# Query and key projections of a head as seven half-size products, with their weight sums on GpSimd and VectorE

## The reference, cut to what matters

```python
h = rms_norm(x, norm_mix)
proj = h @ w_in                       # queries, keys, values, z of 16 heads, and more
qkv_c = silu(causal_depthwise_conv(qkv_buf, qkv, dn_conv_w))
q, k, v = (t.reshape(b, l, DN_HEADS, DN_HEAD_DIM) for t in jnp.split(qkv_c, 3, axis=-1))
# per head: gated delta rule over q, k, v; its output, normed and gated by z, goes on
```

## Time and profile before

| | |
|---|---|
| median of three runs | 3596.15 us (3595.7 to 3596.55) |
| the profiled execution's own time | 3597.47 us |
| its span, first to last instruction | 3595.4 us |
| TensorE busy in the span | 3049.1 us (85%) |
| VectorE, ScalarE, GpSimd busy | 1676.9, 689.1, 455.0 us |
| mean granted clock of TensorE | 0.844 |

### The profile page before, as it was taken

The page is one execution under the profiler, slowest core; times in us unless marked ns, Lnnn a source line. Parts: engine busy times, 40 slices in busy tenths (PEclk is TensorE's granted clock), DMA queues, the critical chain, the costliest instruction groups (busy, mean ns, idle before and its releaser), DMA issues.

```text
span 3595.4 us, 48830 instructions
## 1 busy us (share of the span) xinstructions
PE 3049.1 (85%) x17508; PEld 2001.2 (56%) x17508; DVE 1676.9 (47%) x4076; ACT 689.1 (19%) x1900; POOL 455.0 (13%) x539
## 2 busy tenths in 40 slices
PE   8999999999998999999999999788655666666565
PEld 7766776776776799998887888565100000000000
DVE  4496554555455100026333333468845444444544
ACT  1002343334343100011111111121211111111111
POOL 1000101010000000012111111123311111111111
PEclk9999999999999999999999999889655555555555
DMA  5434433343333788878999999999999999999998
GB/s 222 141 125 151 126 123 124 124 126 124 123 124 109 279 294 293 290 257 346 418 410 407 421 408 413 423 420 411 406 418 413 424 423 424 422 424 423 418 424 362
DMA packets 159446, 1097.43 MB, mean 305 GB/s; under 512 B 22948, under 2 KB 66084, under 8 KB 72892
## 3 DMA queue, kind: packets, MB, share of 16 engines
q0 software_dynamic: 46080, 671.11, 44.5%
q1 hardware_dynamic: 106236, 403.18, 31.6%
q10 hardware_dynamic: 7024, 21.70, 1.5%
HBM read 1064.19 MB, written 31.67 MB: 305 GB/s over the span
## 4 chain that ended last, share of the span: by engine, by line
PE 55%; DMA 27%; DVE 8%; issue 5%; ACT 2%; POOL 1%; SPq 1%; ACTq 0%; DVEq 0%; POOLq 0%
PE psum L572 30%; DMA kv<-in_peer_uv,idx 19%; PE psum L661 12%; PE psum L1073 5%; DMA out_delta_s<-ring_mm 3%; DVE kv L2118 2%; DMA kv<-in_peer_uv,shared 2%; DVE branches L1585 2%; DMA ring_mm<-in_qkv_in 1%; PE psum L740 1%; PE psum L1051 1%; DMA branches<-in_peer_uv,shared 1%; DMA ring_mm<-in_peer_uv,shared 1%; PE psum L728 1%; DMA ring_mm<-in_w_outp 1%
## 5 line engine op out<-in xcount | busy, mean ns | idle before, releaser
L572 PE MATMUL psum<-hT,ring_mm 128*128 128x128 f32 (+2 forms) x4736 | 791.5, 328 | 25.6 <-DMA ring_mm<-in_w_glu 12.0
L572 PEld LDWEIGHTS psum<-hT,ring_mm 128*128 128x128 f32 x4736 | 708.7, 195 | 100.7 <-issue 31.5
L1051 PE MATMUL psum<-shared,selb 32*128 32x512 bf16 x1280 | 298.3, 522 | 415.0 <-DVE dots L2118 415.0
L661 PE MATMUL psum<-hT,ring_mm 128*128 128x320 f32 x2112 | 638.3, 437 | 0.0
L1051 PEld LDWEIGHTS psum<-shared,selb 32*128 32x128 bf16 x1280 | 55.3, 96 | 975.9 <-DVE dots L2118 879.7
L2118 DVE CUSTOM_DVE_ANT_0 ring_mm<-ring_mm,psum 128x1024 f32<-128x1024 f32 x320 | 377.9, 1218 | 369.8 <-DMA ring_mm<-in_peer_uv,idx 244.8
L661 PEld LDWEIGHTS psum<-hT,ring_mm 128*128 128x128 f32 x2112 | 374.1, 190 | 131.5 <-issue 15.1
L1420 ACT ACTIVATE ge<-dots 128x1 f32<-128x1 f32 x320 | 94.3, 295 | 1342.2 <-DVE dots L2118 1333.3
L572 PE MATMUL psum<-branches,ring_mm 128*128 128x128 f32 (+1 forms) x2048 | 292.8, 301 | 1.2 <-issue 1.2
L2118 DVE CUSTOM_DVE_ANT_0 kv<-kv,psum 128x1024 f32<-128x1024 f32 x160 | 189.0, 1219 | 207.9 <-DMA kv<-in_peer_uv,idx 120.2
L572 PEld LDWEIGHTS psum<-branches,ring_mm 128*128 128x128 f32 x2048 | 283.4, 191 | 4.7 <-issue 4.7
(11 more groups left out here) (454 smaller groups left out, 2609.7 us busy)
## 6 DMA issues: line engine op xcount, KB each, us to landing
ring_mm<-in_w_merge SPq DMA_DIRECT2D x160, 1024.0 KB, 5.3
ring_mm<-in_w_head SPq DMA_DIRECT2D x64, 1024.0 KB, 5.7
ring_mm<-in_w_outp SPq DMA_DIRECT2D x32, 1024.0 KB, 7.3
ring_mm<-in_w_pq SPq DMA_DIRECT2D x32, 1024.0 KB, 9.4
ring_mm<-in_w_att SPq DMA_DIRECT2D x24, 1024.0 KB, 5.5
ring_mm<-in_w_mem SPq DMA_DIRECT2D x16, 1024.0 KB, 4.9
ring_mm<-in_w_glu SPq DMA_DIRECT2D x16, 1024.0 KB, 5.8
out_qkv_out<-ring_mm ACTq DMA_DIRECT2D x16, 520.5 KB
```

The costliest lines, as they stand in the source:

```text
L572: last = mat(out, ring[:, j, (k0 + kt) * P:(k0 + kt + 1) * P], src[:, kt, :], start=kt == 0, stop=kt == kts - 1)
L661: last = mat(ps[j][:, 0:TOKENS], ring[:, j, kt * P:(kt + 1) * P], hT[:, kt, :], start=kt == 0, stop=kt == KT - 1)
L1051: last = mat(ps[q][:, :], selb[32 * q:32 * q + 32, j, :], hb[32 * q:32 * q + 32, g_, :], start=True, stop=True)
```

## The change

Queries and keys of a head are no longer two projections of 16 matmuls with 320 tokens. The weights of both are cut into halves of the contraction (`q_lo`, `q_hi`, `k_lo`, `k_hi`, 128x1024 each), the tokens into halves of 160, and the four blocks of the result come from seven products of 8 matmuls with 160 tokens (56 in all, for 32 before). For this four sums of activations are made once (`xsum`, in the place of `xT`, which is loaded again later), and four sums of weights for each head: VectorE adds `wsum = k_lo + k_hi` and replaces `k_lo` by `q_lo - k_lo`; GpSimd replaces `q_lo` by `wsum - q_lo` and `q_hi` by `q_hi - q_lo`. The first product must be copied out (`first_in` on ScalarE) before the third is added to its place. VectorE joins the products (`pair_joined`, eight instructions), ScalarE copies one (`pair_in`); the windows of queries and keys, six copies of ScalarE before, fall away but for that.

`fill(n)` now counts 2n half pieces: one of the products is one, a matmul of 320 tokens two. `KEYS_TO_TURN` is 12.

```diff
+                def pair(k):
+                    n, kt = k // HK, k % HK
+                    w, x, bank, at_, need = (
+                        (q_lo, hT[:, 0:HK, 0:HT], 0, 0, 0), (k_hi, xsum[:, 3, :, :], 1, 0, 0), (q_hi, hT[:, HK:KT, 0:HT], 0, 0, 0),
+                        (wsum, xsum[:, 0, :, :], 1, HT, 1), (k_lo, xsum[:, 2, :, :], 1, 2 * HT, 2),
+                        (q_lo, xsum[:, 1, :, :], 0, HT, 3), (q_hi, hT[:, HK:KT, HT:], 0, 2 * HT, 4))[n]
...
+                        if n == 2:
+                            pe.wait_ge(first_read, PAST + nxt + 1)
+                        if need:
+                            pe.wait_ge(wsum_ready, PAST + 4 * nxt + need)
...
@@ ScalarE, in head(h, nxt), behind the vb copies
+                if nxt is not None:
+                    first_in(nxt)
                 act.wait_ge(tiles_done, FIRST["head"] + 4 * h + 4)
                 act.wait_ge(o_done, h)
                 fn(zs, ps[3][:, 0:TOKENS], ACT.Tanh, scale=0.5).then_inc(z_ready, 1)
-                if nxt is not None:
-                    window(nxt, 0)
@@ VectorE, behind the GLU convolution, and in head(h, nxt)
             raw, beta = uh(sp3[:, 2, :]), uh(sp3[:, 3, :])
+            for n in two:
+                weights_summed(0, n)
...
                     .then_inc(t_ready, 1)
+                if nxt is not None:
+                    weights_summed(nxt, 0)
                 dve.wait_ge(turn_done, h1)
                 v.tensor_copy(tn[:, :, :], three(4)).then_inc(t_ready, 1)
+                if nxt is not None:
+                    weights_summed(nxt, 1)
...
-                        if l == 1:
-                            convolve(nxt, 0, range(2))
-                        if l == 2:
-                            convolve(nxt, 0, range(2, QK))
+                        if l == 3:
+                            pair_joined(nxt)
                         if l == 4:
-                            convolve(nxt, 1, range(2))
+                            convolve(nxt, 0, range(QK))
                         if l == 5:
-                            convolve(nxt, 1, range(2, QK))
+                            convolve(nxt, 1, range(QK))
@@ GpSimd
+            def weights_summed(h):
+                pool.wait_ge(wsum_ready, PAST + 4 * h + 2)
+                pool.wait_ge(prod_done, PAST + 6 * h + 1)
+                g.tensor_tensor(q_lo, wsum, q_lo, ALU.subtract).then_inc(wsum_ready, 1)
+                pool.wait_ge(wsum_ready, PAST + 4 * h + 3)
+                pool.wait_ge(prod_done, PAST + 6 * h + 3)
+                g.tensor_tensor(q_hi, q_hi, q_lo, ALU.subtract).then_inc(wsum_ready, 1)
```

More of the change, by code:

```diff
@@ L215, in build @@
         s1, s2 = view(mmf, at, P), view(mmf, at, P)
+        wsum = view(mmf, at, HK * P)
         at = [0]
@@ L218, in build @@
         sqo = mean[:]
+        xsum = xT[:, :, :].rearrange("p k t -> p (k t)").rearrange("p (f k t) -> p f k t", f=4, k=HK)
+        first_product = lt[:, 0, 0:HT]
+        at = [NBATCH * P + 4 * P]
+        half_sums = [view(six, at, HT) for _ in range(3)]
+        q_lo, q_hi = ring[:, 0, 0:HK * P], ring[:, 0, HK * P:]
+        k_lo, k_hi = ring[:, 1, 0:HK * P], ring[:, 1, HK * P:]
         ab_parts = tt
@@ L1249, in head @@
                 fn(rs[:], rs[:], ACT.Sqrt).then_inc(ort_ready, 1)
-            for j in range(3):
-                window(0, j)
+            pair_in(0)
+            window(0, 2)
             store_window(0)
@@ L1586, in _, with weights_summed, pair_joined, product @@
                 st.leave(4)
+            def weights_summed(h, n):
+                if n == 0:
+                    for j in two:
+                        dve.wait_ge(w_in[j], 16 * (BEFORE["head"][j] + 1) + 16 * h)
+                    if not isinstance(h, int):
+                        dve.wait_ge(prod_done, PAST + 6 * h - 2)
+                    v.tensor_tensor(wsum, k_lo, k_hi, ALU.add).then_inc(wsum_ready, 1)
+                if n == 1:
+                    dve.wait_ge(wsum_ready, PAST + 4 * h + 1)
+                    v.tensor_tensor(k_lo, q_lo, k_lo, ALU.subtract).then_inc(wsum_ready, 1)
+            def pair_joined(h):
+                u2, u3, u4 = half_sums
+                def product(bank, n):
+                    return ps[bank][:, n * HT:(n + 1) * HT]
+                def late(j, total, bank, n):
+                    x = product(bank, n)
+                    v.tensor_tensor(qwin[:, j, QK - 1 + HT:QWIN0], total[:, 0:TP - HT], x[:, 0:TP - HT], ALU.add)
+                    return v.tensor_tensor(qwin[:, j, QWIN0:].rearrange("p (b s) -> p b s", b=NBATCH)[:, :, QK - 1:],
+                                           total[:, TP - HT:].rearrange("p (b s) -> p b s", b=NBATCH),
+                                           x[:, TP - HT:].rearrange("p (b s) -> p b s", b=NBATCH), ALU.add)
+                dve.wait_ge(tiles_done, FIRST["head"] + 4 * h + 2)
+                dve.wait_ge(proj_read[0], h + 1)
+                dve.wait_ge(qst_in, 16 * (h + 1))
+                st(v.tensor_tensor(u2, first_product, product(0, 1), ALU.add))
+                st.wait()
+                st(v.tensor_tensor(u3, u2, product(1, 2), ALU.add))
+                st(v.tensor_tensor(u4, u2, product(1, 1), ALU.add))
+                st.wait()
+                v.tensor_tensor(qwin[:, 1, QK - 1:QK - 1 + HT], u3, product(1, 0), ALU.subtract)
+                late(1, u3, 1, 1)
+                late(0, u4, 0, 2).then_inc(proj_read[1], 1)
             def uh(x):
@@ L2236, in _ @@
                                 slot[:, 0:4].unsqueeze(2).to_broadcast([P, 4, P]), ALU.mult).then_inc(um_ready, 1)
+            weights_summed(0)
+            pool.wait_ge(sp_c, 2)
+            with pool.Fori(0, H - 1) as h:
+                head(h, h + 1)
+            head(H - 1, None)
             def lookup_sums(tk, h):
```

71 lines of the change are left out of this document (60 added, 11 removed).

## The result

| | before | after |
|---|---|---|
| median of 4 runs, us | 3595.93 (3595.47 to 3596.55) | 3716.31 (3714.07 to 3717.72) |
| ratio to before, 95% interval | | 1.0334 (1.0316 to 1.0352) |
| span of the profiled execution, us | 3595.4 | 3712.3 |
| one head of the loop, us | 51.08 | 57.84 |
| first tile of the head stage's chain (L713, now L757), us | 336.0 | 349.9 |

The kernel is slower, as forecast, but by 120 us and not by 77. The predicted time was 3673 with a range up to 3705, so the time lies outside.

A forecast was written before the change was run, and what follows sets the result against it. TensorE's instructions were taken to bound the heads. Fifteen heads at +3.55 us (+53), prologue +10.4, last head +0.7, clock +1.5 and +11 gave +77: 3673 us, range 3618 to 3705.

The forecast's parts named there:

- the clock: TensorE at half clock behind long waits: 1.5 us a fall, in about half of the heads, 11 us (bounds 0 and 22).
- wait C: Each head, TensorE ahead of the states' matmul: VectorE's knm copies wait for GpSimd's whole sum instructions; 3.2 us.
- Rival 2: As forecast, but the clock falls in nearly every head, also by wait A: another 11 to 30 us, 3685 to 3703; chance 0.15.
- wait A: Each head, TensorE ahead of the third product: it waits for ScalarE's copy of the first product; 2.45 us.
- Saving, 1.8 us a head: TensorE's query and key matmuls: 15.5 us a head for 17.2, at 0.138 us per 160-column instruction.
- rival 1: No whole-instruction wait: VectorE and GpSimd share at a lower rate or copies slip in; 3614 to 3636 us; chance 0.17.
- D and E: Later query taps delay a VectorE link, 0.2 us; fewer matmuls left at the head's end, 0.4 us.
- Prologue, 10.4 + 1.5: Before the heads: TensorE stands 10.3 us for VectorE's first sum, first keys +1.9, less 1.8 saved; 1.5 for a clock fall.

The follow-up runs named there:

- The run with quarters: The changed kernel with each of GpSimd's two weight sums cut into four instructions of 256 columns; 3616.98 us, ratio 1.005 to the kernel before.

## Why the prediction was wrong in size

**The step that failed is the clock**, in the prediction's words "wait C (3.2 us) in about half of the heads: 15 x 0.5 x 1.5 = 11, with bounds 0 and 22". It falls behind C in all 15 heads and behind A in 14, and costs 4.0 us a head: 60 us. Rival 2 had the mechanism and ended at 3703; it was also too small. The price of one fall, 1.5 us from the GLU stage, was near the 1.66 measured for a short one. The count was wrong: the GLU stage's wait of 2.21 us without a fall was taken to clear wait A, and "half of the heads" for C was a guess between 2.21 and 2.91. The duration was wrong too: 29 falls at 1.5 us would be 44, and the fall at C lasts twice as long as the other. The rest of the sum was 9 us too high (65.6 for 56.8) and hid a little of it.

The two waits of the GLU stage could not carry that count. In the changed kernel this stage has the same work, and there it is the shorter wait that brings a fall and the longer one that brings none (timeline, then the clock behind each):

```profile
192.28 19.18 PE L584 MATMUL psum<-hT,ring_mm 128*128 128x320 f32 x64 [2.33 <-DMA ring_mm<-in_w_glu]
...
232.38 7.80 PE L584 MATMUL psum<-hT,ring_mm 128*128 128x320 f32 x28 [2.91 <-DMA ring_mm<-in_w_glu]
```

```profile
193.50:196.00 2.50, 2.50 (x6) 1.52 (x6) 2.50 (x10) 0.00 (x0) 0.00 (x0) 0.50 0.45 188
232.00:240.00 8.00, 7.62 (x28) 5.43 (x29) 8.00 (x28) 0.00 (x0) 0.00 (x0) 1.00 0.25 105
```

Point by point:
 - **Saving, 1.8 us a head: right**, and a little small. 16 instructions at full clock take 2.34 us, steps of 0.136 to 0.138 each; with waits A and C gone TensorE's busy time is 2.1 us less than before, of which 1.6 come out in the period.
 - **Wait A, 2.45: right**, 2.14 measured, on the engine and line named.
 - **Wait C, 3.2: right**, 2.94 measured, and 3.5 where A was filled. A copy stood 2.2 us behind GpSimd's instruction. The run with quarters shows that it is a wait for a whole instruction, so rival 1 is out.
 - **D and E, 0.6: not paid.** The wait in level 5 is 0.44 as before, and at the end of the head TensorE (L742) stands 1.0 us in all 15 heads together. Why these links had more room than reckoned was not tried.
 - **Sum of these: forecast 3.55, measured 2.76** with the clock held up; x15 this is 53 against 41.
 - **Prologue, 10.4 + 1.5: nearly right**, 13.9. TensorE reached the wait 3 us earlier (its third product starts at 289.25 for 292.53, the GLU stage's last load having come earlier), so it stood 13.4 us for 10.3. The held-up `tensor_scalar` were not foreseen; they cost nothing here, but once the first wait was filled they were 4.3 of the 8.5 us that TensorE stood for that chain.
 - **Clock, 11: wrong**, 60.

In sum 41.4 + 60.1 + 13.9 + 1.5 = 116.9 of span, against 77.

The costs do not add up when taken one by one. Taking away A gave 5.7 us a head, taking away C 6.8, both 8.4. Each removal takes part of the other's clock with it. The runs show that the length of a wait doesn't decide alone: the same 2.23 us brings a fall in every head where the other wait stands 8 us behind, in every second one where C is removed, and in 5 of 14 with the quarters; and in the GLU stage 2.33 us brought one and 2.91 none. What else decides is open; a wait of a chosen length between stretches of full work wasn't tried. So that the clock makes the 60 us is shown, and how often it falls is only counted.

## What to carry to other kernels

When TensorE is 98% busy, price a new wait of 2 us or more as the wait plus about 2 us for a stretch at half clock behind it, and ask what it would be if that came every time: one wait elsewhere that passed without a fall doesn't clear it; filling both with useless matmuls is a quick test that separates the clock from the wait. Before sums go to GpSimd, list VectorE's SBUF-only instructions that will be issued while one runs, and put the long sum behind the ones that someone waits for, or cut it up. An algebraic saving of 1.8 us in 51 is worth having only if the order of issue is made anew around it: here the same seven products gave +3.3% as first ordered and -0.5% with three changes of order and GpSimd's sums cut up.

## What the runs showed of the hardware

 - A VectorE instruction that reads one SBUF tensor and constants (`tensor_scalar`, 48 columns, 0.19 us) was held for 2.31 and 2.34 us while GpSimd ran sums of 2.35 and 2.46 us. The `tensor_tensor` and the copy just ahead of it (0.20 each) were not; they had begun 0.16 and 0.04 us before GpSimd's sum.
 - GpSimd's sum of two SBUF inputs of 1024 columns takes 2.36 us, of 256 columns 0.73.
 - TensorE's clock fell to 0.50 behind a wait of 2.23 us in every head but the first (whose wait is 0.85) in the changed kernel, in every second head in the one without wait C, in 5 of 14 heads (2.24) in the one with quarters, and not behind the GLU stage's 2.21; behind waits of 2.02 in 4 of 14 heads; in the changed kernel's GLU stage behind one of 2.33 and not behind one of 2.91.
 - A half-clock stretch can cost less than its own loss: behind A the 16 instructions of product 3 took 1.6 us longer and L757 0.2, but wait C was 0.6 us shorter than in the run without this stretch.
